# Prompt attention of a hybrid decoder step: a unit's transposes put behind the value products of the unit before it

## What is computed

```python
p_c = masked_softmax(einsum('bqghd,bngd->bghqn', qg, kc) * scale, mask_c)
o_c = einsum('bghqn,bngd->bqghd', p_c, vc)
...
p_s = masked_softmax(einsum('bqghd,bgqkd->bghqk', qg, kg) * scale, mask_s)
o_s = einsum('bghqk,bgqkd->bqghd', p_s, vg)
...
p_w = masked_softmax(einsum('bqghd,blgd->bghql', qg, kw) * scale, mask_w)
o_w = einsum('bghql,blgd->bqghd', p_w, vw)
o = g[:, :, 0] * o_c + g[:, :, 1] * o_s + g[:, :, 2] * o_w
```

## Time and profile before

| | |
|---|---|
| runs | 2034.68, 2035.16, 2037.83 us; median 2035.16 |
| the profiled execution's own time | 2033.51 us |
| its span, first to last instruction | 2031.7 us |
| mean granted TensorE clock | 0.935 |
| busy over the span: PE, VectorE, ScalarE, POOL | 1778.6, 712.9, 578.6, 361.6 us |
| prompt attention, first scores to last coefficient products | 389 to 701 us of the span |

### The profile page before, as it was taken

The page is one execution under the profiler, slowest core; times in us unless marked ns, Lnnn a source line. Parts: engine busy times, 40 slices in busy tenths (PEclk is TensorE's granted clock), DMA queues, the critical chain, the costliest instruction groups (busy, mean ns, idle before and its releaser), DMA issues. The chain is left out here.

```text
span 2031.7 us, 26076 instructions
## 1 busy us (share of the span) xinstructions
PE 1778.6 (88%) x11014; PEld 1296.0 (64%) x11014; DVE 712.9 (35%) x1181; ACT 578.6 (28%) x1104; POOL 361.6 (18%) x230
## 2 busy tenths in 40 slices
PE   4899588699898899999886858996999999997698
PEld 3345366466666599999775546873668865553485
DVE  3111111255455475601875224222301114442242
ACT  4001111155444442222453223322411102321221
POOL 1111000011000122322765423110000000002132
PEclk9899898799999999999998779997999999997799
DMA  9010363222120011110000461203101010002631
GB/s 335 19 72 1 107 156 80 69 93 77 43 80 6 6 32 44 51 42 25 1 1 11 119 184 75 73 34 100 42 21 42 21 42 1 1 1 78 217 114 57
DMA packets 116919, 130.63 MB, mean 64 GB/s; under 512 B 16790, under 2 KB 89160, under 8 KB 116676
## 3 DMA queue, kind: packets, MB, share of 16 engines
q1 hardware_dynamic: 103908, 120.49, 18.9%
q10 hardware_dynamic: 12544, 8.39, 1.3%
q0 software_dynamic: 352, 0.10, 0.2%
HBM read 107.84 MB, written 23.18 MB: 64 GB/s over the span
## 5 line engine op out<-in xcount | busy, mean ns | idle before, releaser
L155 PE MATMUL banks<-w_attn,h_T 128*128 128x512 f32 (+5 forms) x432 | 161.6, 537 | 0.0
L155 PE MATMUL banks<-h_T_rest,w_ssd_high 128*128 128x352 f32 x480 | 155.3, 324 | 0.0
L155 PE MATMUL banks<-h_T_high,w_ssd_rest 128*128 128x352 f32 x480 | 154.7, 322 | 0.0
L155 PE MATMUL banks<-h_T_high,w_ssd_high 128*128 128x352 f32 x480 | 154.5, 322 | 0.1
L155 PEld LDWEIGHTS banks<-w_attn,h_T 128*128 128x128 f32 (+1 forms) x432 | 78.9, 184 | 81.4 <-issue 64.6
L155 PE MATMUL banks<-w_r,h_T 128*128 128x512 f32 (+1 forms) x288 | 128.5, 600 | 0.0
L155 PE MATMUL banks<-w_qkv,h_T 128*128 128x256 f32 (+1 forms) x576 | 125.7, 380 | 0.5 <-ACT h_T L2227 0.5
L1133 DVE TENSOR_REDUCE neg_max_att<-banks 128x1 f32<-128x640 f32 (+7 forms) x128 | 88.9, 702 | 83.5 <-PE banks L155 83.1
L155 PEld LDWEIGHTS banks<-w_qkv,h_T 128*128 128x128 f32 (+1 forms) x576 | 103.8, 181 | 22.5 <-issue 2.6
L155 PE MATMUL banks<-h_T,w_qkv 128*128 128x352 f32 x384 | 114.5, 460 | 0.0
L155 PE MATMUL banks<-out_even_w_high,mix_high 128*128 128x512 f32 (+1 forms) x216 | 87.5, 405 | 15.8 <-DVE out_even_w_rest L2025 11.8
(11 more groups left out here) (448 smaller groups left out, 3126.2 us busy)
## 6 DMA issues: line engine op xcount, KB each, us to landing
w_mod_late<-in_w_mod_dram SPq DMA_DIRECT2D x8, 2048.0 KB
w_ssd<-in_w_in_even_dram SPq DMA_DIRECT2D x20, 512.0 KB, 3.9
w_mod_rows<-in_w_mod_dram SPq DMA_DIRECT2D x4, 2048.0 KB, 21.0
w_qkv<-in_w_in_odd_dram SPq DMA_DIRECT2D x8, 1024.0 KB, 5.3
xin<-in_x_prompt_dram SPq DMA_DIRECT2D x8, 512.0 KB, 6.2
page_rows<-in_cache_nsa_dram SPq DMA_DIRECT2D x16, 256.0 KB, 2.7
cmp_w<-in_nsa_cmp_w_dram SPq DMA_DIRECT2D x8, 512.0 KB
state_in<-in_state_ssd_dram SPq DMA_DIRECT2D x8, 512.0 KB, 4.6
```

Source lines behind the costliest of these rows:

```text
L155: return nc.tensor.matmul(out, lhsT, rhs, start=start, stop=stop, skip_group_check=True)
```

## The change

In PE's order the value products of unit n-1 go ahead of the transposes of unit n. Iteration n becomes `scores(n + 1)`, `values(n - 1)`, `turn(n)`. Nothing else differs: the same instructions run on every engine, with the same waits in front of each, and the orders of ScalarE, VectorE, POOL and SP stay. For the last unit `turn` and its own values keep their order. `turn_coef` and `mod_job` now come directly behind `turn(n)`.

```diff
@@ -1049,9 +1049,9 @@
                 for n in range(len(units)):
                     if n + 1 < len(units):
                         scores(n + 1)
-                    turn(n, groups[n])
                     if n:
                         values(n - 1)
+                    turn(n, groups[n])
                     if n + 1 == len(units):
                         values(n)
                     for f in fins[n]:
```

## The result

The changed kernel takes 2085.41 us (median of 4 runs, 2082.37 to 2086.51) against 2035.26 before: a ratio of 1.0242 with the interval 1.0224 to 1.0259, 50 us slower. I had forecast 2070.5 with a range up to 2083. The direction and the mechanism are as forecast, the size is 15 us short.

The account below looks back on a forecast made before the run. The first half was taken as PE-bound, the second as held by waits on exponentials and copies; terms 11.3 + 12.2 + 5.5 + 2.2 + 0.5 + 0.9 + 2.8 = 35.4 us gave 2070.5, range 2058 to 2083.

Parts of the forecast that it names:

- The chain: Large units: later transposes delay copies, the next unit's maximum and exponential, then scores; 1.25 us per plain 5-block iteration.
- the nine plain ones: Nine plain 5-block iterations of the large units: each loses 1.25 us, together 11.3 us.
- Small units: Units up to 4 blocks stay PE-bound; four coefficient blocks and two jobs wait for copies, 2.8 us.
- Behind the stage: The next stage's first products wait for a load issued behind the barrier, so the stage's delay passes on in full.
- The clock: PE's granted clock in the stage's second half stays at 1.00 despite pauses of some 1.8 us before large units' scores.
- The second rival: PE's clock falls in the new pauses before large units' scores: 2082, or 2155 if low throughout; chance 0.07.
- its mild case: Clock 0.93 as in a later stage, 14% of the time at the low level: adds 12 us, 2082.
- the upper bound of the sum: All slack used up, so the whole values' duration is lost in all 34 iterations: 47 us, 50 with small units.
- The scores' wait: PE's wait for ScalarE's exponential before score masks grows from 5.6 to some 45 us, in about 30 waits.
- the third sign: The forecast would be wrong if the clock falls below 0.98 in the stage's second half.
- Faster and no change: Whole kernel: faster by more than 0.2%, chance 0.03; within 0.2%, chance 0.02.
- R and N: Large iterations: R, first transpose to exponential done; N, to next scores; faster needs N above R by the values' duration.

Follow-up runs that it names:

- the kernel with plain fills: Changed kernel plus 6 identity products in pauses before large units' scores, none where the next unit is compressed: 2070.99 us, ratio 1.0178 to the kernel before.
- the repeat: The changed kernel measured once more, nothing altered: 2078.83 us, ratio 1.0201 to the kernel before.
- the kernel with 6 products in the pauses: Changed kernel plus 6 identity products before large units' scores, also at three places where the next unit is compressed: 2073.22 us, ratio 1.0175 to the kernel before.
- the one with heads first: Changed kernel with maxima and exponentials of unit n+1 ahead of the copies of unit n on VectorE and ScalarE: 2041.55 us, ratio 1.0034 to the kernel before.

## Why the prediction was right and wrong

- *The chain.* Right, and to the hundredth in the 5-block iteration; the nine plain ones lose 11.2 us in the kernel with plain fills, where 11.3 were forecast. That kernel has a stage 37.9 us longer than before with 3.4 us at the half clock (1.5 us); that leaves 36.4 for a sum of 35.4.
- *Small units.* 2.8 us forecast, 3.3 measured where they alone were reordered. In the changed kernel's own trace the first 35 iterations are 4.2 longer.
- *Behind the stage.* Passed on in full: 49.9 us in the stage, 50 in the time.
- *The clock.* Here it failed: "So I leave the clock at 1.00." The reasoning set a pause of 1.54 us before, without a fall, against one of 3.32 us with a fall, and put 1.8 us on the side of the first. The runs show that pauses below 2 us do lower it, at some of them: 31 and 38 us at the half clock in two traces of the changed kernel. Against the kernel with plain fills, whose own 3.4 us count too, that is 13.6 and 16.5 us. Before, the 1.54 us stood once; after, PE pauses for 1.2 to 1.9 us in 19 places, and seven stretches at the half clock follow.
- *The second rival* had this at 0.07 and 2082 in its mild case. Its mechanism came in, beside the forecast's, and the two add: 36 and 14 are the 50. I treated it as an alternative of low chance instead of a term. Its size was near (14% of the time at the low level and 12 us, where iterations 35 to 71 have 31 of 245 us, 13%), but by luck, since the share was taken from another stage. The rule of the Trainium skill ("TensorE: Matmul & The Clock Gate", section "A second HAM failure mode: psum-queue depth-cycling") that short, frequent pauses make the clock swing agrees with this trace: 0.94 after, 0.99 with the pauses filled.
- *The range.* How far the time passes it changes with the execution: the eight of the changed kernel lie between 2073.85 and 2086.57, four of them within the range up to 2083, and the repeat's median is 2078.83. That the upper bound of the sum, "50 with the small units", equals the measured 50 is also luck: it stood for slack used up in the chain, and the chain took 36.
- *The signs named in advance.* The scores' wait grew to 34.7 us in 26 places, not to 45 in 30. The first half grew by about 4 us. The second half's clock fell below 0.98, the third sign that it would be wrong.
- *Faster and no change* had 0.05 together and were rightly small: R and N of the earlier trace rows left no room.

## What to carry to other kernels

Where several engines run hand-written orders, a block is not free to move because its own engine has room: read what the other engines' orders put behind its neighbours, and follow the chain once around. A price in idle time on TensorE can have a second part: if the change makes many new pauses, add the clock as a term, priced from rows at either level, rather than as an unlikely case. And a filler in the pause is a cheap way to measure the two parts separately, above all when the two traces are compared iteration by iteration.

## What was not expected of the hardware

PE's 19 pauses of 1.2 to 1.9 us, 6 to 28 us apart, brought the granted clock to the half level for 31 to 38 us of a stage of 355 to 358 us; a single 1.54 us pause in the same stage before did not. In the two traces of the changed kernel the low clock stands in the same nine iterations, and in two more in the repeat; with the large units alone reordered, some places are others (48, 51 and 69, but not 39, 52, 61, 63 and 66). About 1.4 us of useless products in the pauses brought the clock back (0.99) and took the excess over the kernel before from 42 and 50 us to 37.

What exactly makes one pause lower the clock and the next not, these runs leave open. Whether the pauses must repeat is open too: in the kernel with plain fills a single unfilled pause of 1.86 us stands at the fall, while the same pause in the kernel with only the large units reordered has none. Nor is it shown that the clock makes the runs spread. The changed kernel's spread over 13 us and those of the kernel before over 7, but the kernel with 6 products in the pauses spreads over 10.5 and the one with heads first over 14, with 3 us at the half clock in the traced stage of either.
